# Output projection of a hybrid transformer block: three of four units as seven block products, on one Trainium2 core

## What is computed

```python
y_a = (y_a * jax.nn.gelu(gr)) @ w_branch_a[l]
y_b = y_b @ w_branch_b[l]
merged = jax.nn.sigmoid(ga) * y_a + jax.nn.sigmoid(gb) * y_b
x = x + gate1[:, None, :] * (merged @ w_out[l])
h = _modulated_norm(x, norm_ffn_g[l], shift2, scale2)
```

## Time and profile before

| | |
|---|---|
| median of three runs | 1552.59 us |
| the three runs | 1552.23, 1552.59, 1552.94 us |
| span of the profiled execution, first to last instruction | 1551.2 us |
| TensorE busy | 1525.7 us (98%) |
| VectorE, ScalarE, GpSimd busy | 1184.4, 791.9, 376.9 us |

### The profile page before, as it was taken

The page is one execution under the profiler, slowest core; times in us unless marked ns, Lnnn a source line. Parts: engine busy times, 40 slices in busy tenths (PEclk is TensorE's granted clock), DMA queues, the critical chain, the costliest instruction groups (busy, mean ns, idle before and its releaser), DMA issues.

```text
span 1551.2 us, 19444 instructions
## 1 busy us (share of the span) xinstructions
PE 1525.7 (98%) x6856; PEld 1249.5 (81%) x6856; DVE 1184.4 (76%) x1431; ACT 791.9 (51%) x1181; POOL 376.9 (24%) x288
## 2 busy tenths in 40 slices
PE   7999999999999999999999999999999999999998
PEld 4778777788888888888887778888888888888886
DVE  6987988646565684466338999999999987778785
ACT  5368888645554461112224555555555553444446
POOL 0023434422222200000000333333333330233324
PEclk9999999999999999999999999999999999999999
DMA  9431223212332256667211144444444436677722
GB/s 348 175 111 52 89 69 92 82 55 82 109 102 82 100 171 220 197 195 231 95 55 35 48 149 149 158 155 150 150 149 150 152 126 227 241 242 250 243 66 109
DMA packets 199838, 219.54 MB, mean 142 GB/s; under 512 B 8928, under 2 KB 155712, under 8 KB 199104
## 3 DMA queue, kind: packets, MB, share of 16 engines
q1 hardware_dynamic: 199744, 218.32, 42.6%
HBM read 160.61 MB, written 57.67 MB: 141 GB/s over the span
## 4 chain that ended last, share of the span: by engine, by line
PE 76%; DVE 15%; ACT 4%; issue 4%; DMA 1%; POOL 0%; SPq 0%; POOLq 0%; ACTq 0%; DVEq 0%
PE ps L784 53%; PE ps L855 15%; DVE wop L1708 4%; DVE hidw L2217 1%; PE ps L996 1%; PE ps L1086 1%; PE ps L1068 1%; DVE ps L1721 1%; PE ps L940 1%; DVE part_acc L1770 1%; ACT wop L1147 1%; DVE tn L1800 1%; DVE yq L1805 1%; DVE ti L1912 1%; DVE yq L2160 1%
## 5 line engine op out<-in xcount | busy, mean ns | idle before, releaser
L1708 DVE TENSOR_TENSOR wop<-raw,wop 128x512 fp32r<-128x512 f32 (+1 forms) x520 | 378.4, 735 | 169.8 <-ACT wop L1147 167.0
L1147 ACT ACTIVATE wop<-raw 128x512 fp32r<-128x512 f32 (+1 forms) x520 | 293.4, 569 | 404.9 <-PE ps L784 157.2
L784 PE MATMUL ps<-yq,wop 128*128 128x512 f32 x1680 | 405.1, 390 | 1.3 <-DVE wop L1708 0.7
L784 PEld LDWEIGHTS ps<-yq,wop 128*128 128x128 f32 x1680 | 314.3, 188 | 71.2 <-issue 3.8
L628 POOL TENSOR_TENSOR raw<-raw,raw 128x512 f32<-128x512 f32 (+1 forms) x64 | 95.2, 1488 | 880.0 <-DVE wop L1708 593.4
L784 PE MATMUL ps<-dq,wop 128*128 128x512 f32 x840 | 190.9, 389 | 0.5 <-DVE wop L1708 0.5
L784 PEld LDWEIGHTS ps<-dq,wop 128*128 128x128 f32 x840 | 157.5, 188 | 33.6 <-issue 0.9
L784 PE MATMUL ps<-t4q,wop 128*128 128x512 f32 x528 | 128.5, 392 | 1.9 <-DVE ps L1721 1.9
L784 PE MATMUL ps<-t2q,wop 128*128 128x512 f32 x528 | 127.7, 391 | 1.9 <-DVE wop L1708 1.0
L784 PE MATMUL ps<-t3q,wop 128*128 128x512 f32 x528 | 127.9, 391 | 0.8 <-ACT snap_u L1159 0.8
L784 PE MATMUL ps<-t1q,wop 128*128 128x512 f32 x528 | 127.7, 391 | 0.0
(11 more groups left out here) (233 smaller groups left out, 1948.6 us busy)
## 6 DMA issues: line engine op xcount, KB each, us to landing
dq<-hid_keep SPq DMA_DIRECT2D x35, 1024.0 KB, 7.2
raw<-in_w_in SPq DMA_DIRECT2D x96, 256.0 KB, 3.3
raw<-in_w_up SPq DMA_DIRECT2D x96, 256.0 KB, 3.5
hid_keep<-part_b SPq DMA_DIRECT2D x40, 512.0 KB, 3.0
ada_ring<-in_w_ada SPq DMA_DIRECT2D x32, 512.0 KB, 4.2
hid_keep<-part_t SPq DMA_DIRECT2D x20, 512.0 KB, 2.8
raw<-in_w_down SPq DMA_DIRECT2D x80, 128.0 KB, 2.4
ada_w<-in_w_ada SPq DMA_DIRECT2D x8, 1024.0 KB, 11.5
```

What stands on the lines that cost most here:

```text
L784: done = nc.tensor.matmul(bank, left[:, w, lk, :], right[:, x, rk, :], start=(first and w == 0 and x == 0), stop=(last and w == 1), skip_g ...
L1147: nc.scalar.activation(wop[n % 4][:, 0, 0:depth[n], :], raw[slot][:, 0:depth[n], :], ACT.Copy).then_inc(f_hi, 1)
L1708: V.tensor_tensor(wop[n % 4][:, 1, 0:kd, :], raw[slot_of[n][0]][:, 0:kd, :], wop[n % 4][:, 0, 0:kd, :].bitcast(F32), ALU.subtract).then_in ...
```

## The change

Units O0, O1 and O2 become block units. Their right-hand side is merged, cut into blocks by input half (tiles 0 to 3, tiles 4 to 7) and token half. Its four combinations are made once and kept for the three units: to1 = (tiles 0-3, second tokens) - (tiles 0-3, first tokens); to2 = (tiles 4-7, second) - to1; to3 = (tiles 4-7, second) - (tiles 0-3, second); to4 = (tiles 4-7, first) - to2. GpSimd makes to1, to3 and to4 in parts of 2, 2, 3, 1 and 4 tiles of 128x512 (5 instructions), and the weight combinations of the three units (12 instructions); VectorE makes to2 in three parts and the low parts of all four in 7 instructions; ScalarE makes the high parts in 7 instructions. Unit B3 keeps its 96 matmuls in another order: the first four input tiles for both output tiles in turn, then the column sum, then the second four input tiles for tile 6, then for tile 7. The x_keep load is moved behind the making of all combinations and comes in three pieces. The squares move to another buffer (sq_o). O3 stays plain, and the U units are as before, with counters shifted.

```diff
+        to1q, to2q, to3q, to4q = (quad(f"to{i + 1}q", "Y", at * QUAD) for i, at in enumerate((1, 2, 3, 0)))
+        to1w, to3w, to4w = (place(f"to{i}w", [KH, HALF], F32, "Y", at * QUAD + QUAD // 2) for i, at in ((1, 2), (3, 3), (4, 0)))
+        to2w = xT[:, 0:KH, 0:HALF]
+        snap_o1, snap_o5 = (place(n, [HALF], F32, "T", 2 * TILE + i * 4 * HALF) for i, n in enumerate(("snap_o1", "snap_o5")))
+        sq_o = place("sq_o", [S], F32, "T", TILE)
...
-            return item[0] in "ABOML" or item == ("G", 0) or item[0] == "U" and item[1] < PLAIN
+            return item[0] in "ABML" or item in (("G", 0), ("O", 3)) or item[0] == "U" and item[1] < PLAIN
...
-            if item == ("U", 0):
+            if item in (("U", 0), ("B", 3)):
                 return ("A11", "A21", "A12", "A22")
...
-                if SEQ[now] == ("B", 3):
+                if SEQ[now] == ("O", 0):
                     sp.wait_ge(spilled, 16)
-                    sp.wait_ge(mg_lo, KH)
-                    sp.dma_start(xT[:, 0:KH, :], x_keep[:, 0:KH, :]).then_inc(kept_back[0], 16)
-                if SEQ[now] == ("O", 0):
                     sp.wait_ge(mg_lo, KT)
-                    sp.dma_start(xT[:, KH:KT, :], x_keep[:, KH:KT, :]).then_inc(kept_back[1], 16)
+                    sp.wait_ge(u_made, IN_SUMS + 5)
+                    sp.wait_ge(sum_lo, IN_LO + 5)
+                    for i, ks in enumerate((slice(0, 2), slice(2, KH), slice(KH, KT))):
+                        sp.dma_start(xT[:, ks, :], x_keep[:, ks, :]).then_inc(x_landed[i], 16)
...
+            def merged_sum(dst, left, right):
+                nc.gpsimd.tensor_tensor(dst, left, right, ALU.subtract).then_inc(u_made, 1)
+
+            weight_sums(("O", 0), (0,))
+            pool.wait_ge(*used_at[NB3 + 1])
+            pool.wait_ge(mb_done, KH)
+            merged_sum(to1w[:, 0:2, :], xT[:, 0:2, H[1]], xT[:, 0:2, H[0]])
+            merged_sum(to1w[:, 2:KH, :], xT[:, 2:KH, H[1]], xT[:, 2:KH, H[0]])
+            weight_sums(("O", 0), (1,))
+            pool.wait_ge(*used_at[NB3 + 3])
+            pool.wait_ge(mb_done, KT - 1)
+            merged_sum(to3w[:, 0:3, :], xT[:, KH:KT - 1, H[1]], xT[:, 0:3, H[1]])
+            pool.wait_ge(mb_done, KT)
+            merged_sum(to3w[:, 3:KH, :], xT[:, KT - 1:KT, H[1]], xT[:, 3:KH, H[1]])
+            pool.wait_ge(t_made, 3)
+            merged_sum(to4w[:, :, :], xT[:, KH:KT, H[0]], to2w)
+            weight_sums(("O", 1))
+            weight_sums(("O", 2))
...
+            def last_branch(pos):
+                banks, free = BANKS[pos % 2], branch_free(pos)
+                set_free(pos, 0)
+                set_free(pos, 1)
+
+                def branch_tile(s, k):
+                    n = NB3 + 2 * (k // KH) + s
+                    if k % KH == 0:
+                        ready(n)
+                    for w, x in PRODUCTS:
+                        for h in range(2):
+                            done = nc.tensor.matmul(banks[s][:, h, :], wop[n % 4][:, w, k % KH, :], branch_b(k, x, h),
+                                                    start=(k == 0 and w == 0 and x == 0), stop=(k == KT - 1 and w == 1))
+                    if k % KH == KH - 1:
+                        done.then_inc(used, 1)
+
+                for k in range(KH):
+                    for s in range(2):
+                        branch_tile(s, k)
+                free(1)
+                for s in range(2):
+                    for k in range(KH, KT):
+                        branch_tile(s, k)
+
+            last_branch(AT["B", 3])
...
+            def proj_unit(pos):
+                act_t, val_t = BANKS[pos % 2]
+                i, n0, snaps = SEQ[pos][1], first_op[SEQ[pos]], 3 * block_unit[SEQ[pos]]
+                set_free(pos, 1)
+                product7(val_t[:, 0, :], n0, merged_block(0, 0))
+                set_free(pos, 0)
+                if i == 0:
+                    pe.wait_ge(sum_lo, IN_LO + 3)
+                product7(act_t[:, 1, :], n0 + 1, to1q)
+                pe.wait_ge(snapped, snaps + 1)
+                if i == 0:
+                    pe.wait_ge(sum_lo, IN_LO + 5)
+                product7(val_t[:, 0, :], n0 + 2, to2q, True)
+                pe.wait_ge(snapped, snaps + 2)
+                if i == 0:
+                    pe.wait_ge(mg_lo, KT)
+                product7(act_t[:, 1, :], n0 + 3, merged_block(1, 1), True)
+                pe.wait_ge(snapped, snaps + 3)
+                if i == 0:
+                    pe.wait_ge(sum_lo, IN_LO + 6)
+                product7(val_t[:, 0, :], n0 + 4, to3q, True)
+                product7(act_t[:, 0, :], n0 + 5, merged_block(1, 0))
+                pe.wait_ge(joined, snaps + 2)
+                if i == 0:
+                    pe.wait_ge(sum_lo, IN_LO + 7)
+                product7(val_t[:, 0, :], n0 + 6, to4q, True)
...
+                if SEQ[pos] == ("O", 0) and i == 0:
+                    act.wait_ge(mb_done, KT)
...
+            def to_high(dst, src, sums, n):
+                act.wait_ge(sums, n)
+                nc.scalar.activation(dst, src, ACT.Copy).then_inc(sum_hi, 1)
...
+            hi(NB3 + 3)
+            merged_high(4)
+            merged_high(5)
+            hi(NB3 + 4)
+            hi(NB3 + 5)
+            to_high(to1q[:, 0, 0:2, :], to1w[:, 0:2, :], u_made, IN_SUMS + 1)
+            to_high(to2q[:, 0, 0:2, :], to2w[:, 0:2, :], t_made, 1)
+            to_high(to1q[:, 0, 2:KH, :], to1w[:, 2:KH, :], u_made, IN_SUMS + 2)
+            hi(NB3 + 6)
+            merged_high(6)
+            to_high(to2q[:, 0, 2, :], to2w[:, 2, :], t_made, 2)
...
+            for i in range(3):
+                pos = AT["O", i]
+                n0 = first_op["O", i]
+                for w in range(7):
+                    if w in (1, 2, 3):
+                        snap(pos, w - 1)
+                    if i == 0 and w == 1:
+                        to_high(to2q[:, 0, 3, :], to2w[:, 3, :], t_made, 3)
+                        merged_high(7)
+                    if i == 0 and w == 3:
+                        to_high(to3q[:, 0, :, :], to3w[:, :, :], u_made, IN_SUMS + 4)
+                    if i == 0 and w == 5:
+                        to_high(to4q[:, 0, :, :], to4w[:, :, :], u_made, IN_SUMS + 5)
+                    hi(n0 + w + 3)
+                    if i and w in (0, 1):
+                        proj_square(2 * i - 2 + w)
+            proj_square(4)
+            hi(N3 + 3)
+            proj_square(5)
...
+            def to2_part(*ks):
+                part = slice(ks[0], ks[-1] + 1)
+                dve.wait_ge(u_made, IN_SUMS + (1 if ks[-1] < 2 else 2))
+                dve.wait_ge(mb_done, KH + ks[-1] + 1)
+                V.tensor_tensor(to2w[:, part, :], xT[:, KH + ks[0]:KH + ks[-1] + 1, H[1]], to1w[:, part, :], ALU.subtract)\
+                 .then_inc(t_made, 1)
+
+            def to_low(dst, src, high, n):
+                dve.wait_ge(sum_hi, IN_HI + n)
+                V.tensor_tensor(dst, src, high.bitcast(F32), ALU.subtract).then_inc(sum_lo, 1)
+
+            gate_b(5)
+            lo(NB3 + 3)
+            merged_low(4)
+            merged_low(5)
+            lo(NB3 + 4)
+            lo(NB3 + 5)
+            mod_part(3, BANKS[(AT["B", 3] - 1) % 2][0])
+            to2_part(0, 1)
+            to_low(to1q[:, 1, 0:2, :], to1w[:, 0:2, :], to1q[:, 0, 0:2, :], 1)
+            dve.wait_ge(sum_lo, IN_LO + 1)
+            to_low(to2q[:, 1, 0:2, :], to2w[:, 0:2, :], to2q[:, 0, 0:2, :], 2)
+            to_low(to1q[:, 1, 2:KH, :], to1w[:, 2:KH, :], to1q[:, 0, 2:KH, :], 3)
+            gate_b(6)
+            to2_part(2)
+            lo(NB3 + 6)
             gate_b(7)
+            to2_part(3)
+            to_low(to2q[:, 1, 2, :], to2w[:, 2, :], to2q[:, 0, 2, :], 4)
+            to_low(to2q[:, 1, 3, :], to2w[:, 3, :], to2q[:, 0, 3, :], 5)
+            merged_low(6)
...
+            def proj_evict(pos, s):
+                i = SEQ[pos][1]
+                m = 2 * i + s
+                if s:
+                    dve.wait_ge(*used_at[first_op[SEQ[pos]] + 6])
+                dve.wait_ge(joined, 3 * block_unit[SEQ[pos]] + (2 if s else 3))
+                dve.wait_ge(x_landed[i], 32)
+                V.scalar_tensor_tensor(xT[:, m, :], flat(BANKS[pos % 2][s]), g1h[:, m:m + 1], xT[:, m, :], ALU.mult, ALU.add)\
                  .then_inc(x2_ready, 1)
...
+            for i in range(3):
+                pos = AT["O", i]
+                n0 = first_op["O", i]
+                for w in range(7):
+                    if w >= 4:
+                        join(pos, w - 4)
+                    if i and w == 0:
+                        proj_evict(pos - 1, 1)
+                    if i == 0 and w == 3:
+                        to_low(to3q[:, 1, :, :], to3w[:, :, :], to3q[:, 0, :, :], 6)
+                    if i == 0 and w == 5:
+                        to_low(to4q[:, 1, :, :], to4w[:, :, :], to4q[:, 0, :, :], 7)
+                    lo(n0 + w + 3)
+                    if i == 0 and w == 0:
+                        merged_low(7)
```

(12 more changed lines are left out.)

96 lines of the change are left out of this document (37 added, 59 removed).

## The result

| | before | after |
|---|---|---|
| median of the runs | 1552.94 us (1552.23 to 1553.68, 5 runs) | 1563.75 us (1560.82 to 1563.95, 5 runs) |
| profiled execution: time, span | 1552.59, 1551.2 us | 1561.16, 1559.4 us |
| granted clock, mean | 0.999 | 0.993 |

The ratio of the runs is 1.0063, with a 95% interval of 1.0052 to 1.0074: the change costs 0.6%. The five runs after lie in two groups, 1560.82 and 1561.16, and 1563.75, 1563.82 and 1563.95. The profiled execution is of the first group. By the medians the change costs 10.8 us, by the ratio 9.8.

A forecast was written before the change was run, and what follows sets the result against it. TensorE, busy 98% of the span, bounds the kernel. -8.2 + 10.8 + 0.2 + 2.7 + 1.0 + 0.8 = +7.3 us takes the span from 1551.2 to 1558.5; the median lies 1.4 higher, 1559.9 us, range 1551.5 to 1563.5.

The forecast's parts named there:

- Saved, 8.2 us: O0 to O2 drop from 96 to 84 matmuls each, 36 x 0.2267 = 8.2 us less TensorE time.
- B3's order, nothing: B3 keeps its 96 matmuls and column sum, so O0 can still start at 738.4: no cost.
- The exclusion, and its lengths: GpSimd and VectorE instructions with two SBUF inputs exclude each other; O0's third product starts 10.8 us late.
- The walk: Instruction-by-instruction timing through B3 and O0, GpSimd going next whenever it waits; 14.7 us of waiting in O0.
- Fourth, 0.2: O0's fourth product waits for the low part of tile 7 and starts at 757.6, 0.2 us late.
- Fifth, 2.7: O0's fifth product waits for to3's low part, starting at 763.0 instead of 760.3: 2.7 us.
- Seventh, 1.0: O0's seventh product waits for to4's low part, ready at 769.4 against 768.4: 1.0 us.
- What is moved, O1 and O2, nothing: Moved x load, O1's weights, O3's tail and added work in O1 and O2 cost nothing.
- The clock, 0.8: O0's 10.8 us stall may halve the clock for the third product: 0.8 us, the middle of 0 and 1.6.
- they fit beside each other: Same work with no exclusion; O0 waits 3.4 us against 8.2 saved, so -4.8 us, 1547.8; chance 0.13.
- VectorE ahead at the hand-overs: VectorE passes before waiting GpSimd in O0, once or always: +3.0 to +4.5 us, 1555.6 to 1557.1; chance 0.17.
- It runs on: O0's backlog delays x or weights, O1 waits, or the clock stays low: +9 to +12 us; chance 0.07.

The follow-up runs named there:

- run 12: Changed kernel with O0 plain, sums on VectorE, loads reordered and the first two tiles' squares one weight part earlier: 1547.97 us, ratio 0.9968 to the kernel before.
- run 1: Kernel before with only B3's matmuls in the new order and the buffers moved: 1553.11 us, ratio 1.0001.
- Run 3: Changed kernel with each of GpSimd's five merged sums replaced by memsets taking as long or longer, reading nothing: 1548.74 us, ratio 0.9972.
- run 6: The changed kernel again, unaltered, beside the other follow-up kernels: 1562.60 us, ratio 1.0061 to the kernel before.
- runs 2: Changed kernel with GpSimd writing zeros in place of the five merged sums, reading nothing: 1550.46 us, ratio 0.9983.
- run 5: Changed kernel with GpSimd's to4 sum waiting until merged is fully split into low parts: 1561.16 us, ratio 1.0046.

## Why the prediction was right, and where it was short

The predicted time was 1559.9 us, in a range of 1551.5 to 1563.5; the profiled execution took 1561.16, and the median of five runs is 1563.75, 3.9 above the forecast and a quarter of a microsecond above the range. The side, the mechanism and most of the size were right. Measured against its own kernel before, the profiled span grew by 8.2 us and the median by 10.8, for a forecast of 7.3.

- **Saved, 8.2 us.** Right. Block products keep 2.72 us, and run 12 shows the saving whole where nothing waits: 5.44 us for 24 matmuls.
- **B3's order, nothing.** Right (run 1).
- **The exclusion, and its lengths.** Right. The walk had tile 7 at 747.2 and it was done at 747.2; the third product at 754.7, and it started at 754.73. Holds of 2.3, 2.3, 3.35, 1.15 and 4.4 us were taken. The rows show 3.3 for the three-tile sum (3.99 less 0.69), 1.1 for the one-tile sum (1.78 less 0.69) and 4.1 for the four-tile sum (5.59 less 1.47). Run 3 shows that it is GpSimd's reading that does it. One hand-over went the other way than walked: the one-tile sum (747.30) went ahead of to2 of tile 7 (747.33), not behind it. That cost nothing, as the same instructions had to be over before the to4 sum either way.
- **Fourth, 0.2.** The low part of tile 7 came at 757.4 as walked, but the slow third product hid it; what is recorded is that product's length.
- **Fifth, 2.7.** Measured 2.68 ahead of it, but at 765.39 and not 763.0; 3.22 in run 6. That the first of these is so near is partly luck: both ends moved by more than 2 us.
- **Seventh, 1.0.** Measured 0.47.
- **What is moved, O1 and O2, nothing.** Right: 38.08 us for both.
- **The clock, 0.8, between 0 and 1.6.** This is the term that was mis-sized. O0 ended at 772.2 in the walk without it and at 774.25 in the trace: 2.0 us, and 3.6 in run 6, where O0 takes 37.43 us. Two things in the step failed. It let the wait for to3 take back 1.1 us; but to3's high part comes behind the snapshot of the slow third product (it ends at 760.83, walked for 758.3), so nothing is taken back. And it allowed for one fall, while the 2 to 3 us ahead of the fifth product let the clock fall again in part of the runs. That second fall is most of what parts the two profiled runs (run 6); of the five runs of the result it is inferred, since only one has a trace here. Against the forecast, then: in the profiled run the clock took about 1.2 us more than its 0.8, and the stretch after O3 had begun gave 0.4 back (747.1 us for 747.5); in run 6 it took 2.8 more.

Of the rivals, *they fit beside each other* is what runs 2 and 3 made by force: 1550.5 and 1548.7, 2.7 and 0.9 above the 1547.8 that it was given (its four waits add up to 3.5, not the 3.4 written); with the sums as they are, it did not happen. *VectorE ahead at the hand-overs* did not happen ahead of the to4 sum, but nor was it put to the test there: the sum stood waiting from 749.19, and the second low part was at hand only at 749.8, when ScalarE had its high part done, with the sum under way. Its arithmetic is tested by run 5, where the third product starts at 750.9, against 750.3 in the text, and the time should have fallen to about 1557: it didn't, since the fifth product and the clock took it. *It runs on*, at 1561.6 to 1564.6 and a chance of 0.07, named the clock staying low through the fourth and fifth product. Three of five runs lie in that span of time; what run 6 shows is near to it, a clock that came back and fell again at the fifth. It deserved more: one row of 0.82 said that the clock falls when TensorE idles, and the sum itself had four stalls.
